# Gated linear attention by pairs of 128-token tiles, without a recurrent state

## The chip, the cores and the metric

The program runs on one core of a Trainium2 chip. The metric is the device time of one execution in microseconds (us). The median of three runs of the kernel before is 1885.37 us (1883.28 to 1887.68).

Each core has a matrix engine (TensorE, PE in the rows; its weight loads are PEld), a vector engine (VectorE, DVE), an activation engine (ScalarE, ACT), a general engine (GpSimd, POOL) and a queue that issues transfers (SyncE, SP). They run their own instruction streams and wait for each other on semaphores. Matrix products go to PSUM, which has eight banks of 128 x 512 f32.

## The reference

A block of two mixers (gated linear attention, then sparse attention), each with a norm and a gated side input, and a second block of five small mixers follow one another. Only the first mixer, gated linear attention, is touched. It has 512 tokens, 4 heads, 256 key columns and 512 value columns in a head, chunks of 64 tokens:

```python
G = jnp.cumsum(g, axis=2)                    # log decay, within a chunk of 64
q_t = q * (GLA_DK ** -0.5) * jnp.exp(G)
k_t = k * jnp.exp(-G)
k_s = k * jnp.exp(G_last - G)
A = jnp.where(tril, jnp.einsum('bnihd,bnjhd->bnhij', q_t, k_t), 0.0)
o_intra = jnp.einsum('bnhij,bnjhv->bnihv', A, v)
def step(S, inp):
    q_c, k_c, v_c, decay = inp
    o_c = jnp.einsum('bihd,bhdv->bihv', q_c, S)
    S = S * decay[..., None] + jnp.einsum('bjhd,bjhv->bhdv', k_c, v_c)
    return S, o_c
o = o_intra + o_inter                        # o_inter: the o_c of all chunks
o = o * lax.rsqrt(jnp.mean(o * o, axis=-1, keepdims=True) + NORM_EPS)
return (o * gn_g * jax.nn.silu(z)) @ w_out   # z: another 2048 columns of x @ w_in
```

## The kernel before

`phase_gla` (L414 to L730) computes this mixer up to the gated result; `phase_post` multiplies it by `w_out`. All activations stay in SBUF. The weights stream in chunks of 1 MB through a ring of two slots: SP loads a chunk (`load_chunks`), ACT copies it to a rounded high part (`split_high`, L156), POOL subtracts to get a low part (`split_low`, L165), and PE multiplies in three products (`split_product`: high by high, high by low, low by high). A slot's high part may be overwritten only when PE has used the chunk two before, so ACT waits in `split_high` for that.

The phase runs in stages, all in PE's program order:

- v: values in token order, 16 blocks of 512 columns; the decay gates are computed in between. DVE makes the cumulative log decay `decay_log`. ACT turns it into `qT = exp(G)`, `kT = exp(-G)` and the chunk ends `chunk_decay` (L610 to L617), one feature block `f` of 128 at a time, and in this loop it also splits weight chunks, for which it waits.
- q and k: for n = 0 to 15, feature block n of q (n < 8) or k. Six PSUM banks rotate: from n = 6 on, PE waits until DVE has used bank n - 6 (`qk_used`). DVE multiplies q by exp(G) (L675). For k it makes two versions, `kT` and the key decayed to its chunk's end, `to_end` (L687, L688). The latter must be in token order for the state update, so PE transposes it (`turn_ks`, L491 to L497) one block later, and ACT copies it (L621).
- attention, L503 to L552: over four tiles j of 128 tokens. For a tile, PE makes the 128 x 128 scores of the four heads (only the two 64 x 64 blocks on the diagonal survive DVE's mask, L694) and multiplies them by v. For each of the two chunks of a tile and each head it adds q times the state (two products of 64 tokens by 512 columns), and makes two products of 64 tokens' keys by 512 value columns that update the state; DVE decays and adds them (L705, 48 times, and 8 plain copies, L703). ACT squares each finished output for its norm and copies it to `v_tok` (L642, L643).
- z: 16 blocks of 512 columns, with all four output banks free; ACT applies silu (L652), DVE multiplies `v_tok` by it (L719).
- turning: PE transposes `v_tok` (`split_feature_major_pe`, L241), ACT and DVE make the high and low parts of the feature-major `gT` (L251, L260), 16 blocks, after all of z. Then the phase ends for all engines, and `phase_post` begins.

Products named in f32 (q times k, scores times v, state) take two matmul records each in the trace; those on the rounded parts take one.

## Time and profile before

| | |
|---|---|
| median of three runs | 1885.37 us |
| profiled execution, first to last instruction | 1882.6 us |
| PE busy | 1685.2 us (90%), 9777 matmuls |
| DVE busy | 725.5 us (39%) |
| ACT busy | 521.2 us (28%) |
| POOL busy | 604.0 us (32%) |
| q and k stage | 135 to 227.6 us |
| attention stage | 227.6 to 361.8 us |
| z stage | 361.8 to 453.2 us |
| turning | 453.2 to 467 us |

Busy time of an engine is the union of its instructions. PEclk in the rows is the TensorE clock that was granted, as a share of 2.4 GHz: 1.00 or, when it is lowered, 0.50 (1.2 GHz). Times are counted from the first instruction.

### The profile page before, as it was taken

How to read it: one execution, taken by the hardware profiler on the slowest of the kernel's cores; microseconds unless marked ns; L12 is line 12 of the kernel's file. 1: busy time of each engine (PE TensorE's matmuls, PEld its weight loads, DVE VectorE, ACT ScalarE, POOL GpSimd, SP SyncE). 2: the span in 40 equal slices, each digit the busy share in tenths (PEclk: the TensorE clock that was granted, in tenths of full speed). 3: DMA queues.
4: the chain of work that ended last, by engine and by line, in shares of the span. 5: the costliest groups of instructions: out<-in, count | busy, mean ns of one | idle time of the engine just before them, and what ended most of it. 6: DMA issues, size and time to landing. Idle time of an engine off the chain costs nothing. (4 is left out here: it accounts for less than half of the span.)

```text
span 1882.6 us, 23223 instructions
## 1 busy us (share of the span) xinstructions
PE 1685.2 (90%) x9777; PEld 1352.8 (72%) x9777; DVE 725.5 (39%) x1468; ACT 521.2 (28%) x833; POOL 604.0 (32%) x251
## 2 busy tenths in 40 slices
PE   6999999999997898898898896979999976868999
PEld 6888733598996775586666696879788743457889
DVE  4111233124114243596766215121230175577431
ACT  2353301224121222224344112143322223411211
POOL 5234300043342227442653234113343062220213
PEclk8999999999998998899999898999999967668869
DMA  4222200033331322031111222232233000000103
GB/s 143 85 68 90 90 23 1 0 91 99 137 113 44 103 68 67 26 109 45 45 46 45 95 97 90 68 116 72 68 104 98 23 1 1 1 28 1 60 15 101
DMA packets 116769, 121.06 MB, mean 64 GB/s; under 512 B 14783, under 2 KB 111017, under 8 KB 116410
## 3 DMA queue, kind: packets, MB, share of 16 engines
q1 hardware_dynamic: 109232, 111.90, 18.9%
q10 hardware_dynamic: 7434, 7.69, 1.3%
q8 instruction: 77, 1.26, 0.3%
q14 instruction: 26, 0.21, 0.0%
HBM read 113.28 MB, written 6.29 MB: 64 GB/s over the span
## 5 line engine op out<-in xcount | busy, mean ns | idle before, releaser
L165 POOL TENSOR_TENSOR w_low<-w_ring,w_high 128x2048 fp32r<-128x2048 f32 (+2 forms) x95 | 420.5, 4426 | 1002.1 <-ACT w_high L156 1002.0
L181 PE MATMUL ps<-w_high,xT_high 128*128 128x256 f32 (+1 forms) x1056 | 307.1, 291 | 12.3 <-ACT heads L1519 5.2
L181 PE MATMUL ps<-w_low,xT_high 128*128 128x256 f32 (+1 forms) x1056 | 299.5, 284 | 0.0
L181 PE MATMUL ps<-w_high,xT_low 128*128 128x256 f32 (+1 forms) x1056 | 299.5, 284 | 0.0
L156 ACT ACTIVATE w_high<-w_ring 128x2048 fp32r<-128x2048 f32 (+2 forms) x95 | 174.1, 1834 | 443.9 <-PE ps L181 434.3
L181 PE MATMUL ps<-xT_high,w_high 128*128 128x512 f32 (+3 forms) x624 | 255.0, 409 | 4.6 <-PEq L757 3.7
L181 PE MATMUL ps<-xT_low,w_high 128*128 128x512 f32 (+3 forms) x624 | 251.9, 404 | 0.0
L181 PE MATMUL ps<-xT_high,w_low 128*128 128x512 f32 (+3 forms) x624 | 251.0, 402 | 0.0
L181 PEld LDWEIGHTS ps<-w_high,xT_high 128*128 128x128 f32 x1056 | 203.1, 192 | 20.6 <-issue 14.9
L181 PEld LDWEIGHTS ps<-w_low,xT_high 128*128 128x128 f32 x1056 | 202.9, 192 | 4.0 <-issue 3.8
L181 PEld LDWEIGHTS ps<-w_high,xT_low 128*128 128x128 f32 x1056 | 202.6, 192 | 0.0
L181 PE MATMUL ps<-w_high,gT_high 128*128 128x256 f32 x512 | 145.8, 285 | 6.0 <-PEq L981 3.3
L181 PEld LDWEIGHTS ps<-xT_high,w_high 128*128 128x128 f32 (+3 forms) x624 | 117.6, 189 | 39.4 <-issue 7.3
L181 PE MATMUL ps<-w_high,gT_low 128*128 128x256 f32 x512 | 145.6, 284 | 0.0
L181 PE MATMUL ps<-w_low,gT_high 128*128 128x256 f32 x512 | 145.5, 284 | 0.0
L181 PEld LDWEIGHTS ps<-xT_high,w_low 128*128 128x128 f32 (+3 forms) x624 | 117.3, 188 | 32.3
L181 PEld LDWEIGHTS ps<-xT_low,w_high 128*128 128x128 f32 (+3 forms) x624 | 117.3, 188 | 30.4
L181 PEld LDWEIGHTS ps<-w_high,gT_high 128*128 128x128 f32 x512 | 99.0, 193 | 6.4 <-issue 6.4
L181 PEld LDWEIGHTS ps<-w_low,gT_high 128*128 128x128 f32 x512 | 99.0, 193 | 0.0
L181 PEld LDWEIGHTS ps<-w_high,gT_low 128*128 128x128 f32 x512 | 99.0, 193 | 0.0
L860 DVE SCALAR_TENSOR_TENSOR x<-x,ps 128x512 f32<-128x512 f32 x16 | 11.0, 687 | 169.8 <-PE ps L181 169.8
L181 PE MATMUL ps<-branch_room 128*128 128x128 f32 (+4 forms) x232 | 52.3, 373 | 11.8 <-DVE fox_peak L1819 5.2
(488 smaller groups left out, 2532.0 us busy)
## 6 DMA issues: line engine op xcount, KB each, us to landing
w_ring<-in_gla_w_in_dram SPq DMA_DIRECT2D x24, 1024.0 KB, 5.5
w_ring<-in_dsa_w_in_dram SPq DMA_DIRECT2D x19, 1024.0 KB, 5.2
w_ring<-in_w_in_dram SPq DMA_DIRECT2D x18, 1024.0 KB, 5.2
w_ring<-in_gla_w_out_dram SPq DMA_DIRECT2D x8, 1024.0 KB, 5.2
w_ring<-in_ple_gate_w_dram SPq DMA_DIRECT2D x8, 1024.0 KB, 5.0
w_ring<-in_dsa_w_out_dram SPq DMA_DIRECT2D x8, 1024.0 KB, 5.0
w_ring<-in_w_out_dram SPq DMA_DIRECT2D x8, 640.0 KB, 4.5
x_scratch<-x SPq DMA_DIRECT2D x4, 1024.0 KB, 7.8
```

The costliest lines, as they stand in the source:

```text
L156: self.nc.scalar.activation(self.w_high[:, i % RING, 0:k, 0:cols], self.w_ring[:, n % RING, 0:k, 0:cols], ACT.Copy).then_inc(self.w_high_m ...
L165: self.nc.gpsimd.tensor_tensor(self.w_low[:, i % RING, 0:k, 0:cols], self.w_ring[:, n % RING, 0:k, 0:cols], self.w_high[:, i % RING, 0:k, ...
L181: return self.nc.tensor.matmul(out, lhs, rhs, start=first, stop=last, skip_group_check=not check)
L860: nc.vector.scalar_tensor_tensor(out=r[:, j, cols], in0=x[:, j, cols], scalar=ALPHA, in1=ps[:, i, :], op0=ALU.mult, op1=ALU.add).then_inc( ...
```

## The change

The recurrent state goes. The 512 x 512 lower triangle of scores of a head is made in full, by pairs (j, i) of 128-token tiles with j <= i, and the output of tile i is the sum over j of scores(j, i) times v(j). The decay between tiles is put into the operands by DVE: `k_on` is the key decayed to the end of its 128-token tile, `q_on` the query grown from the start of its tile, and `q_far` the query with the decay of the one or two tiles between as well. Within a tile the two diagonal 64 x 64 blocks are made as before, and the block of the later half's queries with the earlier half's keys is a 64 x 64 product of its own (`k_mid`), copied into the masked tile.

On PE, q and k now rotate over four banks, and banks 4 to 7 belong to the scores. `scores(h)` of heads 0 to 2 follow k blocks 11, 13 and 15, `outputs(0)`, `scores(3)` and `outputs(1)` to `outputs(3)` come after them. z uses banks 4 to 7 and no longer waits for the last output copy; the transposes of the first 12 gated blocks are put between its blocks. `turn_ks`, its copies, the state and DVE's 56 updates go. Before its first q block DVE waits for all 24 decay instructions and makes three small tensors (`onward`, `tile_decay`).

The core of the diff follows. Blocks of removed lines, which the listing above shows, are left out, as are renamed constants and the same `ks` argument of the helpers on ACT and DVE; the lines are shifted left by eight spaces.

```diff
+def split_feature_major_pe(g, pe, before, src, nk, nt, banks, ks=None):
+    for k in range(nk) if ks is None else ks:
...
+sq = qT[:, 0, :]
+k_on, q_on = mix_b[:, 0:NF, 0:AHEAD * P], mix_b[:, NF:2 * NF, 0:AHEAD * P]
+k_mid = mix_b[:].rearrange("p (r f) t -> p r f t", r=2)[:, :, :, AHEAD * P:]
+q_far = g.alias("q_far", [P, DT, AHEAD, P], F32, room_at)
+near = kT.rearrange("p (h e) t -> p h e t", e=DT)
+extra = w_a2_room[:].rearrange("p (h a) -> p h a", h=GLA_HEADS)
+pair_at = {(0, 1): (1, 0), (0, 2): (1, 1), (0, 3): (1, 2), (1, 2): (1, 3), (1, 3): (2, 0), (2, 3): (2, 1)}
...
+def weights(j, i, h):
+    if j == i:
+        return near[:, h, 0, j * P:(j + 1) * P]
+    which, n = pair_at[j, i]
+    return (near[:, h, 1, :] if which == 1 else extra[:, h, :])[:, n * P:(n + 1) * P]
+def query(f, j, i):
+    if i == j + 1:
+        return q_on[:, f, (i - 1) * P:i * P]
+    return q_far[:, f % DT, {(0, 2): 0, (1, 3): 1, (0, 3): 2}[j, i], :]
...
+        def scores(h):
+            pe.wait_ge(sem["k_on"], past["k_on"] + DT * (h + 1))
+            pe.wait_ge(sem["k_mid"], past["k_mid"] + DT * (h + 1))
+            pe.wait_ge(sem["q_far"], past["q_far"] + 2 * DT * (h + 1))
+            if h:
+                pe.wait_ge(sem["near_masked"], past["near_masked"] + h)
+                pe.wait_ge(sem["middle_copied"], past["middle_copied"] + h)
+                pe.wait_ge(sem["far_copied"], past["far_copied"] + 2 * h)
             for j in range(NT):
-                ins = nc.tensor.transpose(ps[:, 6 + f % 2, j * P:(j + 1) * P], to_end[:, f % 2, j * P:(j + 1) * P], g.ident[:])
-            ins.then_inc(sem["ks_turned"], add("ks_turned", 1))
+                tile = slice(j * P, (j + 1) * P)
+                for d in range(DT):
+                    f = DT * h + d
+                    g.product(ps[:, 4, tile], kT[:, f, tile], qT[:, f, tile], d == 0, d == DT - 1)
+                later = slice(j * P + C, (j + 1) * P)
+                for d in range(DT):
+                    f = DT * h + d
+                    g.product(ps[0:C, 7, j * C:(j + 1) * C], k_mid[:, j // 2, f, (j % 2) * C:(j % 2 + 1) * C], qT[:, f, later], d == 0, d == DT - 1)
+            for (j, i), (which, n) in pair_at.items():
+                for d in range(DT):
+                    f = DT * h + d
+                    ins = g.product(ps[:, 4 + which, n * P:(n + 1) * P], k_on[:, f, j * P:(j + 1) * P], query(f, j, i), d == 0, d == DT - 1)
+            ins.then_inc(sem["scores_ready"], add("scores_ready", 1))
+        def outputs(h):
+            pe.wait_ge(sem["middle_copied"], past["middle_copied"] + h + 1)
+            pe.wait_ge(sem["far_copied"], past["far_copied"] + 2 * h + 2)
+            for i in reversed(range(NT)):
+                if h:
+                    pe.wait_ge(sem["o_copied"], past["o_copied"] + 2 * (NT * (h - 1) + NT - i))
+                for j in range(i + 1):
+                    ins = g.product(ps[:, i, :], weights(j, i, h), v_tok[:, j, h * GLA_DV:(h + 1) * GLA_DV], j == 0, j == i)
+                ins.then_inc(sem["o_ready"], add("o_ready", 1))
         for n in range(2 * NF):
             if n % 2 == 0:
                 w = g.chunk(pe, c_q + n // 2)
-            if n >= 6:
-                pe.wait_ge(sem["qk_used"], past["qk_used"] + n - 5)
+            if n >= 4:
+                pe.wait_ge(sem["qk_used"], past["qk_used"] + n - 3)
             for k in range(KD):
-                ins = g.split_product(ps[:, n % 6, :], columns(w, k, slice((n % 2) * P, (n % 2 + 1) * P)), columns(g.xT, k), k == 0, k == KD - 1)
+                ins = g.split_product(ps[:, n % 4, :], columns(w, k, slice((n % 2) * P, (n % 2 + 1) * P)), columns(g.xT, k), k == 0, k == KD - 1)
             ins.then_inc(sem["qk_ready"], add("qk_ready", 1))
             if n % 2 == 1:
                 g.release("qk_ready")
...
+                if n - NF >= 3:
+                    scores((n - NF - 3) // 2)
         pe.wait_ge(sem["qk_used"], past["qk_used"] + 2 * NF)
...
+        outputs(0)
+        scores(GLA_HEADS - 1)
+        for h in range(1, GLA_HEADS):
+            outputs(h)
...
-                    if half == 0 and n < 4:
-                        pe.wait_ge(sem["o_copied"], past["o_copied"] + 2 * 16)
-                    elif half == 0:
+                    if half == 0 and n >= 4:
                         pe.wait_ge(sem["z_silu"], past["z_silu"] + n - 3)
                     for k in range(KD):
-                        ins = g.split_product(ps[:, n % 4, half * CHUNK:(half + 1) * CHUNK], columns(g.xT, k, slice(j * P, (j + 1) * P)),
+                        ins = g.split_product(ps[:, 4 + n % 4, half * CHUNK:(half + 1) * CHUNK], columns(g.xT, k, slice(j * P, (j + 1) * P)),
                                               columns(w, k), k == 0, k == KD - 1)
                     ins.then_inc(sem[done], add(done, 1))
+                    if c and half == 1:
+                        if j == 0:
+                            pe.wait_ge(sem["gated"], past["gated"] + 4 * c)
+                            pe.wait_ge(sem["o_copied"], past["o_copied"] + 2 * 16)
+                        split_feature_major_pe(g, pe, 0, v_tok, KI, NT, [0, 1, 2, 3], [4 * (c - 1) + j])
                 g.release(done)
         pe.wait_ge(sem["gated"], past["gated"] + 16)
-        split_feature_major_pe(g, pe, 0, v_tok, KI, NT, [4, 5, 6, 7])
+        split_feature_major_pe(g, pe, 0, v_tok, KI, NT, [0, 1, 2, 3], range(KI - 4, KI))
...
+        def pairs_copy(h):
+            act.wait_ge(sem["scores_ready"], past["scores_ready"] + h + 1)
+            nc.scalar.activation(near[:, h, 1, :], ps[:, 5, :], ACT.Copy).then_inc(sem["far_copied"], add("far_copied", 1))
+            nc.scalar.activation(extra[:, h, :], ps[:, 6, 0:2 * P], ACT.Copy).then_inc(sem["far_copied"], add("far_copied", 1))
+        def o_copy(h):
+            for i in reversed(range(NT)):
+                m = NT * h + NT - 1 - i
+                n = NT * i + h
+                act.wait_ge(sem["o_ready"], past["o_ready"] + m + 1)
+                if m:
+                    act.wait_ge(sem["o_copied"], past["o_copied"] + 2 * m)
+                nc.scalar.activation(sq, ps[:, i, :], ACT.Square, accum_out=sumsq[:, n:n + 1]).then_inc(sem["o_copied"], add("o_copied", 1))
+                nc.scalar.activation(v_tok[:, i, h * GLA_DV:(h + 1) * GLA_DV], ps[:, i, :], ACT.Copy).then_inc(sem["o_copied"], add("o_copied", 1))
...
+            if f >= 3 and f % 2 == 1:
+                g.split_high(act, c_q + 6 + (f + 1) // 2)
+                pairs_copy((f - 3) // 2)
+        o_copy(0)
+        pairs_copy(GLA_HEADS - 1)
         g.split_high(act, c_z + RING)
...
+        for h in range(1, GLA_HEADS):
+            o_copy(h)
...
+            nc.scalar.activation(z_silu[:, n % 2, :], ps[:, 4 + n % 4, :], ACT.Silu).then_inc(sem["z_silu"], add("z_silu", 1))
+            if n >= 4:
+                split_feature_major_act(g, act, 0, gT, KI, [0, 1, 2, 3], scale=g.col("gla_gn_g"), ks=[n - 4])
...
+        dve.wait_ge(sem["decays"], past["decays"] + 3 * NF)
+        dve.wait_ge(sem["onward_ones"], past["onward_ones"] + 1)
+        by_tile = chunk_decay[:].rearrange("p f (j b) -> p f j b", b=2)
+        on = onward[:].rearrange("p f r (j b) -> p f r j b", b=2)
+        nc.vector.tensor_copy(on[:, :, 0, :, 0], by_tile[:, :, :, 1]).then_inc(sem["onward"], add("onward", 1))
+        nc.vector.tensor_copy(on[:, :, 1, :, 1], by_tile[:, :, :, 0]).then_inc(sem["onward"], add("onward", 1))
+        nc.vector.tensor_tensor(tile_decay[:], by_tile[:, :, :, 0], by_tile[:, :, :, 1], ALU.mult).then_inc(sem["tile_decay"], add("tile_decay", 1))
+        dve.wait_ge(sem["onward"], past["onward"] + 2)
+        dve.wait_ge(sem["tile_decay"], past["tile_decay"] + 1)
+        halves = lambda x: x.rearrange("p (a i) -> p a i", i=C)
         for n in range(NF):
             dve.wait_ge(sem["qk_ready"], past["qk_ready"] + n + 1)
-            dve.wait_ge(sem["decays"], past["decays"] + 3 * n + 3)
-            nc.vector.scalar_tensor_tensor(out=qT[:, n, :], in0=ps[:, n % 6, :], scalar=GLA_DK ** -0.5, in1=qT[:, n, :],
+            nc.vector.scalar_tensor_tensor(out=qT[:, n, :], in0=ps[:, n % 4, :], scalar=GLA_DK ** -0.5, in1=qT[:, n, :],
                                                              op0=ALU.mult, op1=ALU.mult).then_inc(sem["qk_used"], add("qk_used", 1))
+            dve.wait_ge(sem["qk_used"], past["qk_used"] + n + 1)
+            nc.vector.tensor_tensor(halves(q_on[:, n, :]), halves(qT[:, n, P:]), onward[:, n, 1, 2:].unsqueeze(2).to_broadcast([P, 2 * AHEAD, C]), ALU.mult).then_inc(sem["q_on"], add("q_on", 1))
+        def far_queries(h):
+            dve.wait_ge(sem["q_on"], past["q_on"] + DT * (h + 1))
+            if h:
+                dve.wait_ge(sem["scores_ready"], past["scores_ready"] + h)
+            for d in range(DT):
+                f = DT * h + d
+                nc.vector.tensor_tensor(q_far[:, d, 0:2, :], q_on[:, f, P:].rearrange("p (a i) -> p a i", i=P), tile_decay[:, f, 1:3].unsqueeze(2).to_broadcast([P, 2, P]),
+                                        ALU.mult).then_inc(sem["q_far"], add("q_far", 1))
+            for d in range(DT):
+                f = DT * h + d
+                dve.wait_ge(sem["q_far"], past["q_far"] + 2 * DT * h + d + 1)
+                nc.vector.tensor_scalar(q_far[:, d, 2, :], q_far[:, d, 1, :], tile_decay[:, f, 1:2], None, ALU.mult).then_inc(sem["q_far"], add("q_far", 1))
...
+        def near_masked(h):
+            dve.wait_ge(sem["scores_ready"], past["scores_ready"] + h + 1)
+            nc.vector.tensor_tensor(near[:, h, 0, :].rearrange("p (j i) -> p j i", i=P), ps[:, 4, :].rearrange("p (j i) -> p j i", i=P),
+                                    g.not_before64[:].unsqueeze(1).to_broadcast([P, NT, P]), ALU.mult).then_inc(sem["near_masked"], add("near_masked", 1))
+            dve.wait_ge(sem["near_masked"], past["near_masked"] + h + 1)
+            nc.vector.tensor_copy(near[0:C, h, 0, :].rearrange("p (j b i) -> p j b i", b=2, i=C)[:, :, 1, :],
+                                  ps[0:C, 7, 0:NT * C].rearrange("p (j i) -> p j i", i=C)).then_inc(sem["middle_copied"], add("middle_copied", 1))
         for f in range(NF):
             n = NF + f
...
+            step = to_end[:, f % 2, :]
+            ends = halves(decay_log[:, f, :])
+            nc.vector.tensor_tensor(halves(step), ends[:, :, C - 1:C].to_broadcast([P, NCH, C]), ends, ALU.subtract).then_inc(sem["rest_log"], add("rest_log", 1))
             dve.wait_ge(sem["qk_ready"], past["qk_ready"] + n + 1)
+            nc.vector.tensor_tensor(kT[:, f, :], ps[:, n % 4, :], kT[:, f, :], ALU.mult).then_inc(sem["kt_made"], add("kt_made", 1))
             dve.wait_ge(sem["rest_decay"], past["rest_decay"] + f + 1)
...
+            nc.vector.tensor_tensor(step, ps[:, n % 4, :], step, ALU.mult).then_inc(sem["qk_used"], add("qk_used", 1))
+            dve.wait_ge(sem["qk_used"], past["qk_used"] + n + 1)
+            dve.wait_ge(sem["kt_made"], past["kt_made"] + f + 1)
+            nc.vector.tensor_tensor(halves(k_on[:, f, :]), halves(step[:, 0:AHEAD * P]), onward[:, f, 0, 0:2 * AHEAD].unsqueeze(2).to_broadcast([P, 2 * AHEAD, C]),
+                                    ALU.mult).then_inc(sem["k_on"], add("k_on", 1))
+            nc.vector.tensor_copy(k_mid[:, :, f, :].rearrange("p r (a i) -> p r a i", i=C),
+                                  step.rearrange("p (r a b i) -> p r a b i", r=2, b=2, i=C)[:, :, :, 0, :]).then_inc(sem["k_mid"], add("k_mid", 1))
+            dve.wait_ge(sem["k_on"], past["k_on"] + f + 1)
+            dve.wait_ge(sem["k_mid"], past["k_mid"] + f + 1)
+            if f % 2 == 1:
+                h = f // 2
+                far_queries(h)
+                if h:
+                    near_masked(h - 1)
+        near_masked(GLA_HEADS - 1)
...
+            if n >= 4:
+                split_feature_major_dve(g, dve, 0, gT, KI, [0, 1, 2, 3], scale=g.col("gla_gn_g"), ks=[n - 4])
...
```

## Rows read from the trace of the kernel before

**Rows 1.** The page's busy time of TensorE: us, share of the span, instructions.
```profile
PE 1685.2 (90%) x9777; PEld 1352.8 (72%) x9777; DVE 725.5 (39%) x1468; ACT 521.2 (28%) x833; POOL 604.0 (32%) x251
```

**Rows 2.** Stages from 135 us: length, busy time (instructions) by engine, PEclk, DMA share, GB/s.
```profile
135.00:158.00 23.00, 22.68 (x97) 18.31 (x98) 2.08 (x3) 12.26 (x22) 9.27 (x2) 1.00 0.30 90
158.00:163.70 5.70, 5.70 (x26) 4.56 (x26) 0.78 (x2) 4.21 (x7) 3.63 (x1) 1.00 0.03 10
163.70:227.60 63.90, 63.90 (x288) 51.62 (x287) 17.01 (x26) 17.44 (x19) 24.11 (x6) 1.00 0.32 98
227.60:361.80 134.20, 128.64 (x329) 46.20 (x327) 45.53 (x63) 21.88 (x52) 4.50 (x1) 1.00 0.03 9
361.80:453.20 91.40, 91.34 (x768) 91.20 (x768) 22.71 (x17) 24.77 (x25) 32.26 (x7) 1.00 0.26 81
453.20:467.00 13.80, 9.87 (x65) 6.76 (x64) 11.38 (x17) 12.44 (x18) 4.55 (x1) 1.00 0.25 79
```

**Rows 3.** Who PE waited for, 227 to 468 us: total, times, longest.
```profile
PE ps L181 <- DVE w_a L694: 3.1, 4, 0.8
```

**Rows 4.** PE in order of time, attention: start, length, instruction, tiles, shape, count.
```profile
230.00 2.02 PE L181 MATMUL ps<-mix_a 128*128 128x128 f32 x16 [0.78 <-ACT mix_b L621]
232.81 3.70 PE L181 MATMUL ps<-v_tok,w_a 128*128 128x512 f32 x8 [0.78 <-DVE w_a L694]
236.44 7.13 PE L181 MATMUL ps<-v_tok,mix_b 64*128 64x512 f32 x16
```

**Rows 5.** DVE's uses of q and k blocks: ns min/median/max, first and last start.
```profile
L675 DVE SCALAR_TENSOR_TENSOR mix_a<-ps,mix_a x8: 692/692/692, 141.2 to 180.4; 128x512 f32<-128x512 f32 x8
...
L687 DVE TENSOR_TENSOR to_end<-ps,to_end x8: 691/692/692, 186.0 to 227.8; 128x512 f32<-128x512 f32 x8
```

**Rows 6.** A product of 64 moving columns on 128 weight columns, in order of time.
```profile
1501.21 2.00 PE L181 MATMUL ps<-heads,branch_room 128*128 128x64 f32 x16 [0.79 <-DVE branch_room L1665]
```

**Rows 7.** ACT, then POOL, in order of time: the end of the decays.
```profile
158.08 1.91 ACT L156 ACTIVATE w_high<-w_ring 128x2048 fp32r<-128x2048 f32 x1 [6.99 <-PE ps L181]
...
162.09 0.20 ACT L617 ACTIVATE chunk_decay<-mix_b 128x8 f32<-128x8 f32 x1
...
160.07 4.63 POOL L165 TENSOR_TENSOR w_low<-w_ring,w_high 128x2048 fp32r<-128x2048 f32 x1 [6.57 <-ACT w_high L156]
```

**Rows 8.** DVE's gating of z (ns min/median/max); POOL and DVE in time; a small operation.
```profile
L719 DVE SCALAR_TENSOR_TENSOR v_tok<-v_tok,rstd,to_end x16: 740/751/3735, 377.5 to 453.9; 128x512 f32<-128x512 f32 x16
...
443.94 4.61 POOL L165 TENSOR_TENSOR w_low<-w_ring,w_high 128x2048 fp32r<-128x2048 f32 x1 [6.36 <-ACT w_high L156]
...
445.36 4.39 DVE L719 SCALAR_TENSOR_TENSOR v_tok<-v_tok,rstd,to_end 128x512 f32<-128x512 f32 x2 [13.49 <-ACT to_end L652]
...
L712 DVE RECIPROCAL rstd<-root 128x16 f32<-128x16 f32 x1 | 0.3, 253 | 1.4 <-ACT root L645 1.4
```

**Rows 9.** PE after two idle times, and the clock around them (columns as in rows 2).
```profile
866.31 3.35 PE L181 MATMUL ps<-dsa_kT,mix_a 128*128 128x384 f32 x4 [4.36 <-DVE peak L1257]
...
866.00:872.00 6.00, 5.69 (x12) 3.56 (x13) 3.19 (x19) 2.78 (x9) 0.00 (x0) 0.50 0.57 175
...
653.08 0.47 PE L181 MATMUL ps<-xT_high,w_high 128*128 128x512 f32 x1 [3.65 <-PEq L757]
...
653.00:658.00 5.00, 4.92 (x15) 3.91 (x16) 0.23 (x1) 0.00 (x0) 0.00 (x0) 0.66 0.39 59
```

**Rows 10.** The turning at the end of z, in order of time.
```profile
453.76 1.90 ACT L156 ACTIVATE w_high<-w_ring 128x2048 fp32r<-128x2048 f32 x1
...
455.56 10.14 ACT L251 ACTIVATE gT_high<-ps,cols 128x512 fp32r<-128x512 f32 x16
...
456.28 10.63 DVE L260 SCALAR_TENSOR_TENSOR gT_low<-ps,cols,gT_high 128x512 fp32r<-128x512 f32 x16 [1.63 <-ACT gT_high L251]
```

**Rows 11.** PE's 17-row gate products, and the clock behind them (columns as in rows 2).
```profile
105.09 4.45 PE L181 MATMUL ps<-aT,w_a 17*128 17x512 f32 x8
...
108.00:114.00 6.00, 6.00 (x23) 4.54 (x22) 0.00 (x0) 5.43 (x10) 4.21 (x1) 0.50 0.10 11
```

More of the change, by code:

```diff
@@ L230, in columns @@
     return [part[:, k, cols] for part in parts]
-def split_feature_major_pe(g, pe, before, src, nk, nt, banks):
+def split_feature_major_pe(g, pe, before, src, nk, nt, banks, ks=None):
     sem, past, add = g.sem, g.sem.past, g.sem.add
     nb = len(banks)
-    for k in range(nk):
+    for k in range(nk) if ks is None else ks:
         if k >= nb:
@@ L242, in split_feature_major_pe, with split_feature_major_act @@
         ins.then_inc(sem["turned_whole"], add("turned_whole", 1))
-def split_feature_major_act(g, act, before, dst, nk, banks, scale=None):
+def split_feature_major_act(g, act, before, dst, nk, banks, scale=None, ks=None):
     sem, past, add = g.sem, g.sem.past, g.sem.add
-    for k in range(nk):
+    for k in range(nk) if ks is None else ks:
         act.wait_ge(sem["turned_whole"], past["turned_whole"] + before + k + 1)
@@ L251, in split_feature_major_act, with split_feature_major_dve @@
         g.nc.scalar.activation(dst[0][:, k, :], g.ps[:, banks[k % len(banks)], :], ACT.Copy, scale=s).then_inc(sem["turned_high"], add("turned_high", 1))
-def split_feature_major_dve(g, dve, before, dst, nk, banks, scale=None):
+def split_feature_major_dve(g, dve, before, dst, nk, banks, scale=None, ks=None):
     sem, past, add = g.sem, g.sem.past, g.sem.add
-    for k in range(nk):
+    for k in range(nk) if ks is None else ks:
         dve.wait_ge(sem["turned_high"], past["turned_high"] + before + k + 1)
@@ L437, in phase_gla @@
         qT, kT = mix_a[:, 0:NF, :], mix_a[:, NF:2 * NF, :]
-        state = decay_log
+        decay_log = mix_b[:, 0:NF, :]
+        sq = qT[:, 0, :]
[5 more added lines that the diff above has]
+        pair_at = {(0, 1): (1, 0), (0, 2): (1, 1), (0, 3): (1, 2), (1, 2): (1, 3), (1, 3): (2, 0), (2, 3): (2, 1)}
         ps = g.ps
@@ L651, in _ @@
                         act.wait_ge(sem["gated"], past["gated"] + n - 1)
[L652 removed]
+                    nc.scalar.activation(z_silu[:, n % 2, :], ps[:, 4 + n % 4, :], ACT.Silu).then_inc(sem["z_silu"], add("z_silu", 1))
+                    if n >= 4:
+                        split_feature_major_act(g, act, 0, gT, KI, [0, 1, 2, 3], scale=g.col("gla_gn_g"), ks=[n - 4])
                     if n % 4 == 3:
                         g.split_high(act, c_z + n // 2 + 3)
[L655 removed]
+                split_feature_major_act(g, act, 0, gT, KI, [0, 1, 2, 3], scale=g.col("gla_gn_g"), ks=range(KI - 4, KI))
             @block.vector
@@ L677, in _ @@
                 for f in range(NF):
                     n = NF + f
-                    if f >= 2:
-                        dve.wait_ge(sem["ks_turned"], past["ks_turned"] + f - 1)
-                    ends = decay_log[:, f, :].rearrange("p (c i) -> p c i", i=GLA_CHUNK)
-                    nc.vector.tensor_tensor(to_end[:, f % 2, :].rearrange("p (c i) -> p c i", i=GLA_CHUNK),
-                                                               ends[:, :, GLA_CHUNK - 1:GLA_CHUNK].to_broadcast([P, NCH, GLA_CHUNK]),
-                                                               ends, ALU.subtract).then_inc(sem["rest_log"], add("rest_log", 1))
+                    step = to_end[:, f % 2, :]
@@ L688, in _ @@
-                    nc.vector.tensor_tensor(kT[:, f, :], ps[:, n % 6, :], kT[:, f, :], ALU.mult).then_inc(sem["qk_used"], add("qk_used", 1))
-                update = 0
-                for j in range(NT):
-                    dve.wait_ge(sem["attn_ready"], past["attn_ready"] + j + 1)
-                    if j:
-                        dve.wait_ge(sem["intra_done"], past["intra_done"] + j)
-                    nc.vector.tensor_tensor(attn[:], ps[:, 7, :].rearrange("p (h i) -> p h i", h=GLA_HEADS),
-                                                                  g.not_before64[:].unsqueeze(1).to_broadcast([P, GLA_HEADS, P]), ALU.mult).then_inc(sem["attn_masked"], add("attn_masked", 1))
-                    for half in range(2):
-                        c = 2 * j + half
-                        if c == NCH - 1:
-                            continue
-                        for f in range(NF):
-                            dve.wait_ge(sem["update_ready"], past["update_ready"] + update + 1)
-                            if c == 0:
-                                ins = nc.vector.tensor_copy(state[:, f, :], ps[:, 4 + update % 3, :])
-                            else:
-                                ins = nc.vector.scalar_tensor_tensor(out=state[:, f, :], in0=state[:, f, :], scalar=chunk_decay[:, f, c:c + 1],
-                                                                     in1=ps[:, 4 + update % 3, :], op0=ALU.mult, op1=ALU.add)
-                            ins.then_inc(sem["state_ready"], add("state_ready", 1))
-                            update += 1
```

80 lines of the change are left out of this document (9 added, 71 removed).

## The prediction

> **What bounds the kernel now.** I read the busy times first: PE is busy 90% of the span, the others at most 39% [rows 1], so work taken from PE, or idle time given to it, counts. The stages of the first mixer say the same more sharply [rows 2]: in q and k, attention and z, PE is busy nearly all the time at a granted clock of 1.00. Attention takes 134.2 us with only 4.5 us of POOL, and its largest wait is four times 0.8 us for the mask [rows 3]. It is bound by the matmuls themselves, not by the recurrence: DVE, which carries the state, is busy 46 of 134 us. Only in the turning (13.8 us, PE busy 9.9, DVE 11.4) does DVE set the pace.
>
> **Prices on PE.** In time order [rows 4], a run of n matmul records is n - 1 pitches and one latency. With the latency of a short product at about 0.28 us (128 columns) and 0.60 us (512), I get: 128 columns, (2.02 - 0.28)/15 = 0.116 us a record; 512 columns on full weights, (3.70 - 0.60)/7 = 0.443 us; 512 columns on 64 rows, (7.13 - 0.60)/15 = 0.435 us. A 64-row product thus costs as much as a full one. This is where the old form loses: its 112 products with the state and for the state fill half of the array. An f32 product is two records.
>
> **1. Removed.** The whole attention stretch, 134.2 us [rows 2], of which the 56 updates of the state and the 56 products with it take about 112 x 0.435 = 48.7 us each. Six of the eight `turn_ks` lie inside the k blocks. A block takes (180.4 - 141.2)/7 = 5.60 us in q; from the first to the last use in k it is 41.8 us for seven blocks, where 39.2 would be plain [rows 5]: six transposing groups for 2.6 us, 0.43 us each. The other two lie in the 134.2. Removed: 136.8 us. DVE's state updates, the key copies and the masks' waits were beside this or in it and give nothing more. The wait of z for the last copies lies in it as well.
>
> **2. Put in their place.** Scores of a head: 4 tiles x 2 and 6 pairs x 2 products of 128 columns, 20 products, 40 records. Four heads: 160 x 0.116 = 18.6 us. The middle blocks: 4 x 2 products of 64 columns on 64 weight columns a head, 64 records. No row has this shape at full clock. 64 columns on 128 weight columns run at (2.00 - 0.28)/15 = 0.115 us [rows 6], so there it is the weights that pace; that is the upper bound, 7.4 us. If all scales with the columns, 0.058 us, 3.7 us. I take 0.09 us, 5.8 us: the weights are halved too, but something fixed remains. Outputs: 4 heads x (4 + 3 + 2 + 1) = 40 products, 80 records x 0.443 = 35.4 us (34.8 at the lower pitch). Together 59.8 us. 1 and 2 give **-77.0 us**.
>
> **3. A stall before q block 4.** This is the cost that the change adds most plainly. Block 4 needs bank 0, which DVE now frees only after all decays. Block 3 ends at about 158.0, where ACT's split of a weight chunk starts; only behind this split come the last two feature blocks' decays, and they end at 162.3 [rows 7]. Then DVE makes three tensors of 32 to 64 columns, at most 0.25 us each (a 16-column operation took 0.253 [rows 8]), and the product with bank 0, 0.69 us [rows 5]. Without more, PE would go on at 163.6 to 163.8. But POOL's split runs from 160.07 to 164.70 [rows 7], and one of the three is a tensor operation with both inputs in SBUF. The gating operation, also with both inputs in SBUF, usually takes 0.75 us; the one issued at 445.36 while POOL worked from 443.94 to 448.55 belongs to those of up to 3.735 us, that is, it ended about 0.5 us behind POOL [rows 8]. So I let the small product wait for 164.7, and PE go on at 165.8: a stall of 7.8 us (5.6 if it doesn't wait, 8.5 if the three small operations pile up behind POOL). The later q blocks cost nothing: DVE needs about 1.4 us for each, PE 5.6. **+7.8 us.**
>
> The Trainium skill (SBUF — State Buffer, "Who interferes with whom") says that a DVE instruction with two SBUF inputs contends with a GpSimd instruction that reads SBUF, and the later one waits for the whole of the other. By that rule the sum has 7.8 us here, and 5.6 without it; the gating rows agree with it.
>
> **4. The clock behind the stall.** After PE sat idle 4.36 us, the next 6 us ran at 0.50 with PE busy 5.69: about 3 us lost. After 3.65 us of idling, 5 us ran at a mean of 0.66: 5 x 0.34 = 1.7 us lost [rows 9]. An idle time of 7.8 us, part of which the low clock may cover, I put at 2.2 us (1.7 to 3.1; 0 if the fall is over before PE resumes). **+2.2 us.**
>
> **5. Transposes inside z.** 12 groups of four at 0.43 us, the price of the same group between k blocks: **+5.2 us**. The waits ahead of them are for things done long before: `gated` 4c is over soon after the half stage before, and the low part of the block three back. The silu, copy, gate and low part of one block are about 1.3 us on ACT and 1.5 us on DVE in the 3.3 us that PE now takes for a half block. One gate in four waits for POOL for some 3 us; four banks and the 11 us of the next half stage hide that. If they didn't, it would be up to 3 us three times.
>
> **6. Turning at the end.** 13.7 us before, from the end of z to the last low part (456.28 + 10.63 - 453.2) [rows 10]. Now ACT does silu 0.6, the high part of block 11 (10.14/16 = 0.63), the split of a weight chunk 1.9, then four high parts; DVE follows with four low parts of 0.66. The last one ends 0.6 + 0.7 + 1.9 + 0.7 + 4 x 0.67 + latencies = 6.7 us after z. **-7.0 us.**
>
> **7. What stays hidden.** DVE has per head two `k_on` (384 columns), two `k_mid`, four far queries, the mask and a middle copy: none is longer than a 512-column operation, 0.69 to 0.75 us, together some 8 us with the old k work, in the 17 us from one `scores` to the next. Even a wait of 4.6 us for POOL fits. `scores(h)` comes one pair of blocks after its last operand, so 11 us cover it. `far_queries(h)` waits for `scores(h-1)` and holds the next key block's `rest_log` behind it on DVE, and through it ACT's exp; both end about 4 us after those scores, and the next k block ends 5.6 us after. ACT's splits are queued ahead of `pairs_copy`: the split for block 14 waits for block 11, PE then has scores, 12 and 13 to do, some 17 us against 1.9 + 4.6 us. SP's loads wait only for POOL's low parts as before. `outputs(0)` (8.9 us) covers mask, copies and far queries for `scores(3)`, and `outputs(1)` the last mask. ACT's square and copy of an output take 1.4 us, PE makes one in 0.9 to 3.5 us, and four banks smooth this. If this cover fails, it costs what the second rival says.
>
> **Sum.** -77.0 + 7.8 + 2.2 + 5.2 - 7.0 = -68.8 us. On the profiled execution's 1882.6 us this is 1813.8 us; the median of the runs shown lies 2.8 us above that span, so I forecast 1885.4 - 68.8 = **1816.6 us**. The stages behind depend on the end of this phase only and move as a whole.
>
> **Rivals.**
> (a) *The small products pull the clock down.* The 17-row products took 4.45 us and were followed by 6 us at 0.50 with PE busy throughout [rows 11], 3 us lost. The middle products are small as well. For it: it needs no idle time. Against it: they stand between full products, and the 64-row and 64-column products before never lowered the clock (1.00 over 134 us [rows 2]). At 3 us for each of four `scores`: +12, 1828.6 us. The Trainium skill (TensorE: Matmul & The Clock Gate, "What's actually happening") says that the default is the throttled clock and that activity releases it; it agrees with the fall of [rows 11] only if those products were too little activity. Taken for the middle products too it gives 1828.6, else 1816.6.
> (b) *DVE is late for `scores`.* If SBUF operations queue behind POOL more than once per pair of blocks, each of four `scores` waits some 4 us: +16, 1832.6 us. The slack counted in 7 speaks against it.
> (c) *The stall is cheap.* The small operations don't wait for POOL, the clock falls inside the gap, and the middle products cost the lower bound: -2.2 - 2.2 - 2.1 = -6.5, 1810.1 us.
> (d) *Slower than before.* The stall drops the clock and the many short waits keep it at 0.50 until z ends. PE has 67 us of q and k blocks, 60 of attention and 97 of z to do from there, 224 us, and half the clock roughly doubles the array's part. It decides once more than about 69 us of this work run at half: then the gain is gone. All of it would be some +200, near 2015 us. Against it: the falls of the rows are over after 3.4 to 7 us of dense products, and the stage from 163.7 on ran at 1.00 [rows 2, 9, 11].
> (e) *The change doesn't do what it says*, the old work remaining beside the new: the diff leaves no state product, so I give this nothing beyond rounding.
>
> **How the numbers follow.** Forecast 0.68, (a) 0.12, (b) 0.06, (c) 0.11, (d) 0.03. The forecast's own bounds: middle products -2.1 to +1.6, stall -2.2 to +0.7, clock -2.2 to +0.9, outputs -0.6, z up to +3, and the runs' spread of 2 us. The range reaches from just below (c) to (a): 1808 to 1829 us. A change below 0.2%, 3.8 us, can't be told from none here. Faster by more: 0.965; within: 0.005; slower: 0.03.
>
> **What would show it.** The profile after should have no state products; 40 output products (80 records) near 35 us; scores of some 6 us behind k blocks 11, 13 and 15; one idle time of PE of 6 to 8 us about 158 us after the start, ended by DVE's first q product, and a stretch at 0.50 just behind it; z about 96 us long with transposes inside, and 6 to 7 us from its end to the last low part. The forecast is wrong if PE waits for DVE or ACT before a `scores` or `outputs`, if the clock falls during scores, or if the 64-column products cost as much as the large ones.

## The result and the profile after

The changed kernel takes 1821.3 us (median; 1815.8 to 1824.8) against 1884.7 us: a ratio of 0.966, 95% interval 0.964 to 0.968, 63 us less. The forecast was 1816.6 us in a range of 1808 to 1829. The profiled execution spans 1819.8 us, 62.8 less than before (1882.6).

By stage, the answer to [rows 2] (stretch, length, busy time of PE, PEld, DVE, ACT and POOL, PEclk, DMA share, GB/s):

```profile
135.50:158.60 23.10, 22.63 (x96) 17.95 (x96) 0.00 (x0) 12.41 (x22) 9.27 (x2) 1.00 0.30 89
158.60:166.40 7.80, 0.07 (x2) 0.05 (x1) 3.29 (x5) 4.20 (x7) 4.50 (x1) 0.72 0.03 8
166.40:172.30 5.90, 5.90 (x14) 4.64 (x15) 3.91 (x7) 0.00 (x0) 0.00 (x0) 0.50 0.59 179
172.30:249.80 77.50, 77.50 (x387) 63.48 (x387) 34.76 (x60) 16.20 (x17) 22.93 (x5) 1.00 0.23 68
249.80:297.60 47.80, 47.80 (x194) 27.18 (x192) 5.32 (x12) 20.72 (x50) 4.52 (x1) 1.00 0.08 22
297.60:393.40 95.80, 95.80 (x814) 95.74 (x813) 30.02 (x28) 32.97 (x41) 32.25 (x7) 1.00 0.25 78
393.40:402.30 8.90, 2.49 (x21) 2.02 (x19) 4.14 (x6) 5.29 (x7) 4.52 (x1) 0.92 0.01 2
402.30:408.00 5.70, 5.65 (x27) 5.68 (x28) 0.00 (x0) 0.00 (x0) 0.00 (x0) 0.52 0.99 319
```

The rows show the forecast stall (158.6 to 166.4, PE idle), the low clock that began inside it and lasted until 172.3, then 221 us of full PE at 1.00 through blocks, scores, outputs and z, and then a stretch that the forecast did not have: after the phase ends, PE runs at 0.52 for 5.7 us. Whom PE waited for, 130 to 420 us (total, times, longest), the answer to [rows 3]:

```profile
PE ps L181 <- DVE mix_a L702: 7.7, 1, 7.7
PE ps L181 <- PEq L468: 5.4, 1, 5.4
PE ps L241 <- DVE v_tok L763: 1.0, 1, 1.0
```

Only two idle times matter: the stall, and 5.4 us between the phases, which was 2.7 us before. In order of time, one group of scores (head 2) and the outputs behind it, the answer to [rows 4]:

```profile
249.83 0.61 PE L181 MATMUL ps<-mix_a 128*128 128x128 f32 x4
250.37 0.45 PE L181 MATMUL ps<-mix_a,mix_b 128*64 128x64 f32 x4
250.74 0.71 PE L181 MATMUL ps<-mix_a 128*128 128x128 f32 x4
...
253.79 0.71 PE L181 MATMUL ps<-mix_b 128*128 128x128 f32 x4
...
256.57 1.02 PE L181 MATMUL ps<-v_tok,mix_a 128*128 128x512 f32 x2
```

Scores take 256.57 - 249.83 = 6.74 us. Outputs of head 0 run from there to 265.16, 8.59 us; those of heads 1 to 3 from 271.90 to 297.25, 25.35 us.

### The profile page after: what moved, and what is told of

The parts are those of the page before. It is cut to its first block and busy times, and to the rows that moved or that the text cites. A ratio compares the mean times of both kernels' runs of the same rounds, so it can differ in the third digit from the quotient of the medians.

```text
span 1819.8 us, 23128 instructions
## 1 busy us (share of the span) xinstructions
PE 1618.0 (89%) x9729; PEld 1350.9 (74%) x9729; DVE 707.2 (39%) x1460; ACT 519.9 (29%) x833; POOL 604.4 (33%) x251
```

## The experiments

Times below are medians, with the ratio to the kernel before measured beside it and its 95% interval. The runs of one kernel spread over 5 to 18 us, and the mean granted clock goes with them (for the first experiment 0.914 in the run of 1803.7 us and 0.902 in the one of 1817.7), and 1415 us of the span lie behind this phase. So effects of a few microseconds are read from the traces, from place to place, and the times only say whether they agree.

**The stall: take the wait for all decays off the first four q blocks.** DVE makes the product as soon as the block's own decays are there, and only then waits for the rest. `q_grown(n)` waits for `qk_ready` n + 1 and `decays` 3n + 3 and makes the product of q block n; what stands between the lines is the making of the three small tensors:

```diff
+                for n in range(4):
+                    q_grown(n)
                 dve.wait_ge(sem["decays"], past["decays"] + 3 * NF)
...
                 for n in range(NF):
+                    if n >= 4:
+                        q_grown(n)
```

> On the changed kernel, DVE multiplies the first four q blocks before it waits for all decays and makes the three small tensors, each block waiting for its own three decays only. Nothing else is changed. Theory (the wait for all decays costs a stall and, behind it, a fall of the clock): PE's idle time of 7.7 us before q block 4 goes, and the stretch at 0.50 from 162 to 172 us with it, in which block 4 took 8.6 us instead of 5.6; together about 10.7 us less than the changed kernel, 1810.5 us. Rival (only the stall counts, the clock falls somewhere near by anyway): 7.7 us less, 1813.5 us. Rival (the stall moves to the next use of DVE): PE waits before block 5 to 8 instead, no gain, 1821 us.

Measured: 1811.8 us, ratio 0.960 (0.957 to 0.962), and a span of 1809.2 us, 10.6 below that of the changed kernel. PE in the same stretch of this kernel (columns as above):

```profile
158.80:172.00 13.20, 13.20 (x58) 10.60 (x58) 7.21 (x12) 5.74 (x8) 5.02 (x2) 1.00 0.27 81
```

PE is busy all the time at 1.00: stall and fall are gone, and nothing took their place. DVE's first and last use of a q block lie at 141.6 and 180.8 us, 39.2 apart as in [rows 5]. This bears out the first theory, with its number.

**What in the stall is POOL's.** Here all decays are still awaited, but the first q products come ahead of the small tensors:

```diff
                 dve.wait_ge(sem["decays"], past["decays"] + 3 * NF)
+                for n in range(4):
+                    q_grown(n)
...
```

> On the changed kernel, DVE still waits for all decays, but then multiplies q blocks 0 to 3 before it makes the three small tensors. Theory (2.3 us of the stall are one small SBUF copy that waits for POOL's weight split, the rest is the wait for the decays; an operation that reads PSUM and one SBUF tensor doesn't wait for POOL): the first q product starts at about 163 us, PE's idle time is 5.2 to 5.4 us instead of 7.7; the clock still falls behind it. Rival (DVE's start as such is late, whatever it does first): the first q product also takes 2.3 us longer or starts at 165.5, idle time 7.7 us.

Measured: 1817.0 us, 0.961 (0.958 to 0.964). DVE in order of time, first in the changed kernel:

```profile
162.98 2.29 DVE L694 COPY onward<-chunk_decay 128x32 f32<-128x32 f32 x1 [38.47 <-ACT chunk_decay L627]
165.19 0.17 DVE L695 COPY onward<-chunk_decay 128x32 f32<-128x32 f32 x1
165.27 0.18 DVE L696 TENSOR_TENSOR tile_decay<-chunk_decay 128x32 f32<-128x32 f32 x1
165.55 0.69 DVE L702 SCALAR_TENSOR_TENSOR mix_a<-ps,mix_a 128x512 f32<-128x512 f32 x1
```

and POOL beside it there:

```profile
160.73 4.50 POOL L165 TENSOR_TENSOR w_low<-w_ring,w_high 128x2048 fp32r<-128x2048 f32 x1 [6.57 <-ACT w_high L156]
```

then in this experiment, whose trace runs 2.4 us earlier from the start on (POOL last):

```profile
160.58 2.48 DVE L694 SCALAR_TENSOR_TENSOR mix_a<-ps,mix_a 128x512 f32<-128x512 f32 x4 [38.23 <-ACT chunk_decay L627]
162.98 0.17 DVE L701 COPY onward<-chunk_decay 128x32 f32<-128x32 f32 x1
...
158.34 4.54 POOL L165 TENSOR_TENSOR w_low<-w_ring,w_high 128x2048 fp32r<-128x2048 f32 x1 [6.57 <-ACT w_high L156]
```

```profile
PE ps L181 <- DVE mix_a L694: 5.2, 1, 5.2
```

The same copy takes 2.29 us or 0.17 us. The long one began while POOL worked and ended at 165.27, just behind POOL's split (165.23); the short one began at 162.98, when the split was over (162.88). In the eight other kernels with this copy it began beside the split and took 2.30 to 2.42 us. The four products that read PSUM and one SBUF tensor ran beside POOL at their usual price (2.48 us for four), and the idle time fell from 7.7 to 5.2 us. The clock still fell behind it. It was already the copy, with a single SBUF input, that waited; I had put the wait on the third operation, with two. The Trainium skill (SBUF — State Buffer, "Who interferes with whom") names plain copies among what can contend as well, where their operands meet certain conditions. The row of 2.29 us agrees; no run here tries the conditions.

**What the fall of the clock costs.** 32 products of 512 columns into a bank that nobody reads are put into the stall; the wait stays:

```diff
+                    if n == 4:
+                        for r in range(32):
+                            g.product(ps[:, 5, :], g.xT[0][:, r % KD, 0:P], g.xT[0][:, r % KD, :])
                     if n >= 4:
                         pe.wait_ge(sem["qk_used"], past["qk_used"] + n - 3)
```

> On the changed kernel, PE makes 32 products of 512 columns (7.5 us) whose result nobody reads in the stall before q block 4; the wait itself stays. Theory (the low clock behind the stall is the answer to PE's idle time and costs 2.9 us): the granted clock stays at 1.00 from 150 to 400 us, block 4 takes 5.6 us instead of 8.6, all that follows comes 2.9 us earlier, 1818.4 us. Rival (the fall comes from something else, such as the change of bank or of weights): it stays at 0.50 for some microseconds and nothing is gained.

The clock over the stretch, and PE's wait:

```profile
158.00:162.00 4.00, 4.00 (x20) 3.28 (x19) 0.00 (x0) 3.89 (x6) 1.89 (x1) 1.00 0.05 17
162.00:166.00 4.00, 3.51 (x16) 2.62 (x15) 3.52 (x5) 0.32 (x2) 2.72 (x1) 1.00 0.05 7
166.00:172.00 6.00, 6.00 (x27) 4.81 (x27) 4.12 (x8) 0.00 (x0) 0.00 (x0) 1.00 0.56 170
```

```profile
PE ps L181 <- DVE mix_a L705: 0.5, 1, 0.5
```

No fall here; the one between the phases, behind 5.4 us of idling, came as in the changed kernel, so the clock did not stay at 1.00 up to 400 us as I had expected. From DVE's first use of a q block to its last it is 188.5 - 165.0 = 23.5 us, in the changed kernel 191.7 - 165.5 = 26.2: 2.7 us, near the 2.9 expected. The whole time is inconclusive: 1824.6 us, 0.963 (0.959 to 0.968), with runs from 1810.5 to 1828.3.

**The middle products.** They are moved behind the near ones (the 128 x 128 products within a tile) of their head:

```diff
                     for j in range(NT):
...
+                    for j in range(NT):
                         later = slice(j * P + C, (j + 1) * P)
...
```

> On the changed kernel, the 64 x 64 middle products of a head come after all its near products instead of between them, tile by tile. Theory (each change between 128 and 64 weight columns costs PE about 0.1 us, which is why a scores group takes 6.74 us and not 6.1): six changes fewer in each of four groups, 6.1 to 6.3 us a group, 2 us less in all, 1819 us. Rival (the middle products themselves cost 0.13 to 0.15 us a record): a group stays at 6.7 us, 1821 us. Rival (eight small products in a row let the clock fall): granted clock below 1.00 in or behind the groups, +5 to +12 us.

Head 3 in order of time:

```profile
260.38 1.95 PE L181 MATMUL ps<-mix_a 128*128 128x128 f32 x16
262.25 1.15 PE L181 MATMUL ps<-mix_a,mix_b 128*64 128x64 f32 x16
263.33 0.71 PE L181 MATMUL ps<-mix_b 128*128 128x128 f32 x4
...
266.11 1.02 PE L181 MATMUL ps<-v_tok,mix_a 128*128 128x512 f32 x2
```

A group takes 5.73 us instead of 6.74, 4.0 us less in all, twice what I expected; the clock stays at 1.00. A middle record by itself takes (263.33 - 262.25)/16 = 0.068 us, close to my lower bound (0.058). So the products were cheap, and alternating between the two kinds was dear: six changes fewer for 1.01 us, 0.17 us each. Each of these changes is one of shape and also one of PSUM bank (4 and 7), and this experiment doesn't part the two. The next one speaks for the shape: its full products change banks all the time at the plain price. Time: 1814.9 us, 0.962 (0.959 to 0.964).

**Half-filled products, on the kernel before.** Its products with the state and its updates get all 128 rows or columns of the tile:

```diff
-  g.product(ps[rows, h, :], qT[:, DT * h + d, toks], state[:, DT * h + d, :], ...)
+  g.product(ps[:, h, :], qT[:, DT * h + d, tile], state[:, DT * h + d, :], ...)
-  g.product(ps[:, 4 + update % 3, :], ks_tok[rows, j, f * P:(f + 1) * P], v_tok[rows, j, ...])
+  g.product(ps[:, 4 + update % 3, :], ks_tok[:, j, f * P:(f + 1) * P], v_tok[:, j, ...])
```

> On the kernel before, the products with the state compute all 128 tokens of a tile instead of the chunk's 64, and the updates of the state contract over the tile's 128 tokens instead of the chunk's 64 (so both halves of a tile enter each state; the output differs from the reference by this). Number, columns and order of the matmuls stay. Theory (the old form lost because a half-filled product costs as much as a full one): the attention stage stays at 134 us, +1 us at most. Rival (cost goes with rows or weight columns): up to 48 us more in each of the two kinds, 1930 to 1980 us. Second rival (denser work lowers the clock or doubles the weight loads): the stage grows by some us at 1.00 in PEclk.

The output is no longer the mixer's, so only the time is read. Measured: 1875.5 us, 0.992 (0.990 to 0.995): slightly less than before, which neither theory had. In order of time:

```profile
235.15 7.03 PE L181 MATMUL ps<-v_tok,mix_b 128*128 128x512 f32 x16
242.02 1.88 PE L181 MATMUL ps<-mix_b,mix_a 128*128 128x512 f32 x4
243.73 1.88 PE L181 MATMUL ps<-v_tok,mix_b 128*128 128x512 f32 x4
245.45 1.88 PE L181 MATMUL ps<-mix_b,mix_a 128*128 128x512 f32 x4
...
343.22 7.03 PE L181 MATMUL ps<-mix_b,mix_a 128*128 128x512 f32 x16
```

Two products of each kind alternate every 1.71 to 1.72 us; the last row is eight products with the state in a row. The kernel before, at the same places:

```profile
243.50 1.93 PE L181 MATMUL ps<-mix_b,mix_a 128*64 128x512 f32 x4
245.36 1.98 PE L181 MATMUL ps<-v_tok,mix_b 64*128 64x512 f32 x4
247.27 1.93 PE L181 MATMUL ps<-mix_b,mix_a 128*64 128x512 f32 x4
...
353.42 7.08 PE L181 MATMUL ps<-mix_b,mix_a 128*64 128x512 f32 x16
```

There it is 1.86 and 1.91 us where the kinds alternate, but 7.08 us against 7.03 where one kind runs in a row, and 7.13 [rows 4] against 7.03 for the other. From DVE's first q product to ACT's last output copy the stretch falls from 219.9 to 210.9 us. So the premise holds (a half-filled product is no cheaper than a full one). The two kinds alternate 24 times each; at 1.72 us instead of 1.86 and 1.91 this gives 24 x (0.14 + 0.19) = 7.9 of the 9.0 us, so some 8 us of what the old form cost were the changes between its two half shapes.

**The end of the phase.** The last weight split is left to the next phase:

```diff
-                    if n % 4 == 3:
+                    if n % 4 == 3 and n < 15:
                         g.split_high(act, c_z + n // 2 + 3)
```

> On the changed kernel, the split of the weight chunk that ACT puts between the gated blocks and the last high parts (and POOL's low part behind it) is left to the start of the next phase. Theory (the end of the phase is set by POOL's low part, which ends 1.3 us after DVE's last, and by ACT's 1.9 us in front of the last high parts): the next phase's first product comes about 6 us after z ends instead of 9.0, 3 us less; PE's idle time between the phases falls from 5.4 us to about 2.5, and if that is what let the clock fall at 401 us, another 2.7 us: in all 1815.5 us. Rival (the phase's end is set by something else than ACT and POOL): the next phase starts as late as before, 1821 us. Rival (the next phase pays it back, since its second chunk is now split late): PE waits for POOL about one block behind the start, 1820 us.

The end in the changed kernel, in order of time:

```profile
394.59 1.91 ACT L156 ACTIVATE w_high<-w_ring 128x2048 fp32r<-128x2048 f32 x1
...
396.58 4.52 POOL L165 TENSOR_TENSOR w_low<-w_ring,w_high 128x2048 fp32r<-128x2048 f32 x1 [9.09 <-ACT w_high L156]
397.11 2.72 DVE L260 SCALAR_TENSOR_TENSOR gT_low<-ps,cols,gT_high 128x512 fp32r<-128x512 f32 x4 [1.54 <-ACT gT_high L251]
```

DVE ends at 399.83, POOL at 401.10, and the next phase's first product is at 402.35. In the experiment the end is DVE's:

```profile
393.28 2.73 DVE L260 SCALAR_TENSOR_TENSOR gT_low<-ps,cols,gT_high 128x512 fp32r<-128x512 f32 x4 [0.81 <-ACT gT_high L251]
...
396.40 0.35 PE L181 MATMUL ps<-w_high,gT_high 128*128 128x256 f32 x1 [2.57 <-PEq L468]
```

From the last silu to that product it is 6.0 us instead of 8.9, and the idle time 2.6 instead of 5.4. The clock still fell behind it, but for half as long (3.4 instead of 6.8 us, of which 1.4 lay in the idle time), so PE lost 1.7 us by it instead of 2.7; I had expected the whole 2.7 back. Time: 1816.8 us, 0.962 (0.959 to 0.964).

**Turning back at the end.** The transposes, high and low parts of all 16 blocks follow z, as before the change:

```diff
-                            if c and half == 1:
...
-                                split_feature_major_pe(g, pe, 0, v_tok, KI, NT, [0, 1, 2, 3], [4 * (c - 1) + j])
...
+                split_feature_major_pe(g, pe, 0, v_tok, KI, NT, [0, 1, 2, 3])
```

> On the changed kernel, all 16 gated blocks are turned after z again, as before the change; the rest of the change stays. Theory (the interleaved turning brings little: it gives PE 4.4 us more in z and saves 5.4 us at the end, and by making the end's idle time denser in one piece it lets the clock fall behind it, 2.7 us): z takes 91.3 us, the turning 14.4 us to the next phase's first product, no fall of the clock there, 1.7 us less than the changed kernel, 1819.5 us. Rival (my forecast of this part, 1.8 us gained by interleaving, the fall being by chance): 1823 us.

Measured: 1813.1 us, 0.961 (0.958 to 0.964). ACT's silus (ns, first and last start), here and then in the changed kernel:

```profile
L661 ACT ACTIVATE to_end<-ps x16: 597/600/603, 310.4 to 385.9; 128x512 f32<-128x512 f32 x16
```

```profile
L666 ACT ACTIVATE to_end<-ps x16: 597/597/602, 312.5 to 393.5; 128x512 f32<-128x512 f32 x16
```

z is 5.5 us shorter (75.5 against 81.0), the turning 5.5 us longer (385.9 to 400.3 is 14.4, against 8.9), and PE's idle time before the next phase is 2.7 us, with no fall of the clock. That there was no fall is in part chance: the kernel with full products above ends the phase in the same way, and behind its 2.6 us of idling the clock fell, at a loss of some 1.5 us. Interleaving gained nothing here, and brought an idle time behind which the clock fell in every trace. The median is further below the changed kernel than the 1.7 us of the theory; by the trace not more than about 3 us of it are this edit's.

**Three edits together (c1)**: early q products, grouped middle products, the last split in the next phase.

> The changed kernel with three edits together: the first four q products ahead of the small tensors and of the wait for all decays, the middle products grouped, the last weight split left to the next phase. Theory (the three are separate costs): the next phase's first product comes 10.6 + 4.3 + 3 = 18 us earlier than in the changed kernel, about 384.5 us after the start, and the time is about 1803 us. Rival (they share a cover, such as DVE's or ACT's slack before the scores, and shorter scores expose it): PE waits for DVE or ACT before scores or outputs, less than 15 us gained.

Measured: **1799.5 us, ratio 0.952 (0.950 to 0.955)**, the fastest of all and clear of the changed kernel's interval. The next phase's first product comes at 383.0 us, 19.4 earlier; 1.5 of these lie ahead of q block 4, so 17.9 belong to the edits (18 expected). The stage from 180 us on, and PE's waits:

```profile
180.00:384.00 204.00, 200.40 (x1334) 171.41 (x1333) 72.21 (x100) 71.21 (x111) 55.05 (x12) 1.00 0.20 63
```

```profile
PE ps L181 <- PEq L468: 2.6, 1, 2.6
PE ps L241 <- DVE v_tok L771: 1.0, 1, 1.0
```

No new wait. By themselves the three were worth 10.6, 4.0 and 3.0 us: the costs are separate and add.

**The same with the turning at the end**, beside a second measurement of the changed kernel:

> As c1 (early q products, grouped middle products, last weight split in the next phase), and all 16 gated blocks turned after z as before the change. Theory (interleaving is worth nothing in itself, the PE time it adds to z equals what it saves at the end): z takes 5.5 us less to its last silu, the turning about 12.5 us to the next phase's first product instead of 6.0, so that product comes 1 us later than in c1; the clock doesn't fall behind it, which gives back 1 to 2 us: within 2 us of c1, 1798 to 1801 us. Rival (the interleaving was a real gain that only the fall hid): 4 us or more slower than c1.

> The changed kernel as it is, on the same chip as the run beside it. Theory: 1819 to 1823 us, with PE idle 7.7 us before q block 4 and 5.4 us between the phases, and the clock at 0.50 behind each. If a single profile misled me and the fall of the clock between the phases is by chance, this profile won't show it.

Measured: 1803.6 us, 0.957 (0.954 to 0.959), and 1822.1 us, 0.965 (0.962 to 0.968). With the weight split out of its way the interleaving is worth something: from DVE's first q product to the next phase's first product it is 245.3 us, against 242.6 in the version above. I had expected 1 us for these 2.7. The theory that it is worth nothing thus holds only while the split sets the phase's end. The clock fell in both versions for 3.4 us, here behind an idle time of 2.3 us, so the part of the expectation that had no fall failed. The changed kernel repeated its time, both idle times (7.7 and 5.4 us) and both falls.

## Why the prediction was right, point by point

The range, the sign and the mechanism held; the forecast was 4.7 us low. The terms, each from the traces:

| step | forecast, us | measured, us | from |
|---|---|---|---|
| 1 removed | -136.8 | -136.8 | the same rows of before [rows 2, 5] |
| 2 scores | +24.4 | +27.0 | 4 x 6.74 |
| 2 outputs | +35.4 | +33.9 | 8.59 + 25.35 |
| 3 stall | +7.8 | +7.7 | the wait |
| 4 clock behind it | +2.2 | +2.9 | 5.9 us at 0.50 |
| 5 transposes in z | +5.2 | +4.6 | z 96.0 against 91.4 |
| 6 turning, to the next phase's first product | -7.0 | -5.5 | 8.9 against 14.4 |
| clock at the start of the next phase | none | +2.7 | 5.7 us at 0.52 |
| sum | -68.8 | -63.5 | spans: -62.8 |

That the total is off by only 5 us owes something to luck. Outputs and middle products, priced 1.5 and 1.4 us too dear, hid part of the 4.0 us of shape changes in the scores, which the sum had at nothing, as it had the clock between the phases.

**Step 1** was right that the recurrence was bound by PE's matmuls and not by DVE (the stretch became 9.0 us shorter when only PE's products were filled up), and that half-filled products are no cheaper. It took their pitch from a run of one kind and so missed some 8 us for the changes of shape, which the measured 134.2 us contained anyway: the term was right, the reason incomplete.

**Step 2**, the scores, was the first term off: 6.74 us a group, 6.1 forecast. The middle products cost 0.068 us a record and not 0.09. What I had left out was the alternation of shapes, 1.01 us a group, and the trace of before had it: the steps of 1.86 and 1.91 us shown above, where four records at the pitch of [rows 4] would take 1.74. The outputs, at 33.9/80 = 0.424 us a record, ran below both pitches that I had read; the eight records of the row that I took were too few to read one from.

**Step 3** hit the stall and its size, since it set POOL's end against the end of the decays. The operation that waited was the first copy, not the product of two SBUF tensors; the sum is the same.

**Step 4** was in its bounds. That it costs what it costs, and is the answer to the idle time, is shown by the products in the stall: 2.7 us came back.

**Step 5** was 0.6 us high, and its cover held. **Step 6** failed in one point: I followed ACT and DVE to the end of the phase and not POOL, whose low part is queued behind the same split. DVE ended 6.4 us after z, as forecast (6.7); POOL ended 1.3 us later, and the phase with it. POOL's queue belonged in that step as much as DVE's did. From it came the longer idle time between the phases, 5.4 us, and behind that the fall of the clock, 2.7 us, with the scores' 2.6 the largest miss. All six traces with 5.4 us there show the fall; moving the split shortened both. Whether the clock falls behind the 2.3 to 2.7 us of the other six stays open: it did in four and not in two, and the kernel before and the one with full products differ in this with the same end of the phase.

**Step 7** held: no wait of PE for DVE or ACT before scores or outputs, in any version.

Of the rivals, (a) is refuted, as the clock stayed at 1.00 from 172 us to the end of z, and also with the middle products in a row; these runs are 1.1 us long, so what lowered the clock behind the 4.45 us of 17-row products [rows 11] stays open. (b) didn't come. (c) was half true: the middle products were near the lower bound, but the stall was not cheap. (d) and (e) didn't come.

## What to carry to other kernels

It can pay to replace a recurrence by pairwise products when the matrix engine is the bound and its products are half filled: here 112 half-filled and 16 full products of 512 columns gave way to 40 full ones, and 134 us to some 61 us of scores and outputs. This is for four tiles; the pairs grow with the square of their number. When operations are moved to the end of a phase, follow every engine to that end, the one that only prepares weights too. A wait for a whole loop's results, put in front of the first use of one of them, costs the loop's tail: here 10.6 us with the clock behind it, which a change of order in one loop gave back.

## What the runs showed of the hardware

- Alternating matmul shapes cost time: 0.17 us per change between short products with 128 and with 64 weight columns (which also changed the PSUM bank), and 1.86 and 1.91 us for two products of 512 columns when 64-row and 64-column ones alternated, where full ones took 1.72 us. In a row, eight half-filled products took 7.08 and 7.13 us, full ones 7.03. Filling both kinds up to 128 shortened the stretch from 219.9 to 210.9 us while it computed more.
- A small SBUF copy (128 x 32) took 2.29 to 2.42 us beside a weight split on GpSimd (nine traces) and 0.17 us without it (one).
- 64 columns on 64 weight columns, in a row, take 0.068 us a record at full clock, against 0.115 us on 128 weight columns [rows 6].
- The granted clock fell from 1.00 to 0.50 with idle times of PE of 7.7 us (five traces), 5.2 us (one) and 5.4 us (six) each time; behind 2.3 to 2.7 us between the phases it fell in four of the kernels and stayed in two.
